# Latent and context attention of an even layer: two stages or one

## What is computed

```python
def diff_attend(q, k, v, lam):
    s = jnp.einsum('bhmqd,bhmkd->bhmqk', q, k).astype(F32) * (DIFF_DQK ** -0.5)
    p = jax.nn.softmax(s, axis=-1)
    p = p[:, :, 0] - lam * p[:, :, 1]
    return jnp.einsum('bhqk,bhkv->bhqv', p.astype(v.dtype), v)
```

## Time and profile before

| | |
|---|---|
| median of 3 runs | 4137.01 us (4134.11 to 4137.23) |
| profiled execution, its time | 4135.23 us |
| its span in the profile | 4133.4 us |
| TensorE busy | 3705.0 us, 90% of the span |
| VectorE busy | 2066.0 us, 50% |
| ScalarE busy | 872.8 us, 21% |
| GpSimd busy | 1419.3 us, 34% |
| mean granted TensorE clock | 0.945 of full |
| latent attention stage | from 358.6 us of the span |
| context attention stage | to 519.8 us |

### The profile page before, as it was taken

How to read it: one execution, slowest core, us unless ns; L and a number is a source line. 1 busy time by engine, 2 the same in 40 slices (tenths; PEclk the granted TensorE clock), 3 DMA queues, 4 the chain that set the end, 5 groups by cost and what they waited for, 6 DMA issues and landing times. The chain is left out here.

```text
span 4133.4 us, 45791 instructions
## 1 busy us (share of the span) xinstructions
PE 3705.0 (90%) x18442; PEld 2960.2 (72%) x18442; DVE 2066.0 (50%) x3080; ACT 872.8 (21%) x1697; POOL 1419.3 (34%) x612
## 2 busy tenths in 40 slices
PE   7897889999989889968999888888999888888998
PEld 3773467888878688857878466767888566777887
DVE  5796443223456366673233377763133477753132
ACT  2214312100021333301100343511000243511001
POOL 2321043235553100015455222245445222334454
PEclk9998789999999999989999899999999899999999
DMA  4534212212222000012332221123322321213332
GB/s 163 162 124 174 77 41 75 64 53 65 67 57 82 29 1 1 38 53 76 97 95 72 74 71 46 39 74 87 97 88 70 85 57 46 62 52 97 97 92 72
DMA packets 400351, 306.80 MB, mean 74 GB/s; under 512 B 11228, under 2 KB 367782, under 8 KB 399559
## 3 DMA queue, kind: packets, MB, share of 16 engines
q1 hardware_dynamic: 398040, 303.37, 24.4%
q10 hardware_dynamic: 2095, 0.44, 0.1%
HBM read 297.48 MB, written 6.29 MB: 73 GB/s over the span
## 5 line engine op out<-in xcount | busy, mean ns | idle before, releaser
L410 POOL TENSOR_TENSOR low<-raw,high 128x1024 fp32r<-128x1024 f32 (+1 forms) x437 | 1064.7, 2438 | 1437.3 <-DVE high L331 1437.3
L470 PE MATMUL scores<-high 128*128 128x512 f32 (+1 forms) x2464 | 949.2, 385 | 109.0 <-POOL low L410 82.6
L470 PE MATMUL scores<-low,high 128*128 128x512 f32 (+1 forms) x2464 | 935.2, 380 | 0.0
L470 PE MATMUL scores<-high,low 128*128 128x512 f32 (+1 forms) x2464 | 933.4, 379 | 0.0
L331 DVE CAST high<-raw 128x1024 fp32r<-128x1024 f32 (+1 forms) x437 | 414.3, 949 | 691.0 <-PE scores L470 375.9
L470 PE MATMUL bank<-high 128*128 128x512 f32 (+1 forms) x1792 | 666.7, 372 | 36.8 <-POOL low L410 26.9
L470 PE MATMUL bank<-low,high 128*128 128x512 f32 (+1 forms) x1792 | 663.5, 370 | 0.0
L470 PE MATMUL bank<-high,low 128*128 128x512 f32 (+1 forms) x1792 | 662.5, 370 | 0.0
L470 PEld LDWEIGHTS scores<-high 128*128 128x128 f32 x2464 | 475.8, 193 | 211.2 <-POOL low L410 87.8
L470 PEld LDWEIGHTS scores<-high,low 128*128 128x128 f32 x2464 | 473.9, 192 | 88.5
L470 PEld LDWEIGHTS scores<-low,high 128*128 128x128 f32 x2464 | 475.8, 193 | 84.4 <-issue 0.5
(11 more groups left out here) (581 smaller groups left out, 4358.6 us busy)
## 6 DMA issues: line engine op xcount, KB each, us to landing
raw<-in_mlp_w SPq DMA_DIRECT2D x128, 512.0 KB, 4.0
raw<-in_w_in SPq DMA_DIRECT2D x76, 512.0 KB, 3.9
ring<-in_ada_w SPq DMA_DIRECT2D x32, 1024.0 KB, 7.3
raw<-in_w_gate SPq DMA_DIRECT2D x44, 512.0 KB, 4.0
raw<-in_w_up SPq DMA_DIRECT2D x44, 512.0 KB, 3.9
raw<-in_w_down SPq DMA_DIRECT2D x40, 512.0 KB, 3.5
mix<-in_ada_w SPq DMA_DIRECT2D x16, 1024.0 KB, 7.1
raw<-in_od_w_in SPq DMA_DIRECT2D x29, 512.0 KB, 3.9
```

The lines of the kernel that those rows point to most:

```text
L410: pool.tensor_tensor(tile(low, u), tile(raw, u), tile(high, u).bitcast(F32), ALU.subtract)\
L470: mm = pe.matmul(out(p), stationary, moving, start=(k0 + k == 0 and i == 0), stop=(k0 + k == job.kc - 1 and i == len(pairs) - 1))
```

## The change

Both stages become one. Its units are L0 L1 C0 L2 L3 C1 ... L14 L15 C7: a context block behind every second latent block, 24 in all, with the loop order of before (scores one unit ahead, turn one unit behind) over this list. Context weights have tiles of their own (`p_ctx`, `pT_ctx`). The banks are divided anew: latent scores 0 to 3 as before; latent turns in 4 and in the first half of 5; context turns in the second half of 5; both maps of the context scores in bank 6, half each, where the second map's scores wait until the first's are done. The output products of both kinds go to bank 7, which they share with the modulation's products: an output waits until `flat` has been taken, and the modulation's next product waits until the output has been stored. Outputs are due two units after a head's last block. A context block's maxima are taken and scaled in one instruction each for both maps.

The side runs in the latent units only. Units 0 to 11 multiply as before. Unit 12 does nothing; units 13, 14 and 15 each turn four chunks of `flat` (16 products, 32 records) into bank 7, and VectorE adds the bias after each (three times in all). `LaterTurn` is gone. The 24 loads, their queue, their ring and their waits are unchanged.

The core of the diff (where "..." stands in `diff_attention`, the old code was that printed above; everything new is shown):

```diff
--- before.py
+++ after.py
@@ -936,11 +936,6 @@
 class LaterModulation(Modulation):
 
 
-    SIGNALS = Modulation.SIGNALS[:5]
-    TURN_SIGNALS = ("mod_turned", "mod_done")
-
-    def with_signals(self, signals):
-        *self.loaded, self.multiplied, self.taken = signals
 
     def take(self, act, n):
         act.wait_ge(self.multiplied, 2 * n + 2)
@@ -950,48 +945,42 @@
         for n in range(len(self.steps)):
             self.load(sp, n)
 
+    def wait_for_bank(self, pe, blocks):
+
+        n_units = len(self.steps)
+        if blocks:
+            pe.wait_ge(self.taken, min(blocks, n_units))
+        if blocks > n_units + 1:
+            pe.wait_ge(self.done, blocks - n_units - 1)
+
+    def units_of(self, u):
+        n = 4 * (u - len(self.steps) - 1)
+        return range(n, n + 4) if n >= 0 else range(0)
+
+    def outs(self):
+        return self.m.bank[self.banks[0]][:, 0:32].rearrange("p (i s) -> p i s", s=2)
+
     def tensor(self, pe, u):
         if u < len(self.steps):
             self.multiply(pe, u)
+        elif u > len(self.steps):
+            self.wait_for_bank(pe, u)
+            for n in self.units_of(u):
+                for i in range(4):
+                    mm = pe.matmul(self.outs()[:, 4 * (n % 4) + i, :], self.flat[:, n, i * P:(i + 1) * P], self.m.chosen,
+                                   start=True, stop=True)
+            mm.then_inc(self.turned, 1)
 
     def scalar(self, act, u):
         if u < len(self.steps):
             self.take(act, u)
 
     def vector(self, dve, u):
-        pass
-
-
-class LaterTurn:
-
-
-    SIGNALS = LaterModulation.TURN_SIGNALS
...
-            bias = self.m.ada_b[:, self.layer, 0:4 * self.units].unsqueeze(2).broadcast_to([P, 4 * self.units, 2])
-            dve.tensor_tensor(self.mods[:, 0:4 * self.units, :], self.out, bias, ALU.add).then_inc(self.done, 1)
+        if u > len(self.steps):
+            layer, at = self.steps[0][0], slice(4 * self.units_of(u)[0], 4 * self.units_of(u)[-1] + 4)
+            bias = self.m.ada_b[:, layer, at].unsqueeze(2).broadcast_to([P, 16, 2])
+            dve.wait_ge(self.turned, u - len(self.steps))
+            dve.tensor_tensor(self.mods[layer][:, at, :], self.outs(), bias, ALU.add).then_inc(self.done, 1)
 
 
 class FilterSpectra:
@@ -1362,143 +1351,179 @@
                                                   in1=small.norm_g[:, 0, :], op0=ALU.add, op1=ALU.mult))
 
 
-def diff_attention(nc, m, q, k, v, neg_lam, o, queries, keys, side=None):
-
-
-
-    q0, qn = queries
-    k0, kn = keys
-    nq, nk = qn // P, kn // P
+class HeadUnit:
+
+
+
+    def __init__(self, m, latent, n):
+        self.latent, self.n = latent, n
+        self.blocks = (LAT if latent else CTX)[1] // P
+        self.h, self.b = divmod(n, self.blocks)
+        self.q0, self.qn = LAT if latent else CTX
+        self.k0, self.kn = (0, TA) if latent else CTX
+        if latent:
+            self.score_parts = [[(m.bank[2 * mp], 0, 512), (m.bank[2 * mp + 1][:, 0:TC], 512, TC)] for mp in range(2)]
+            self.scores = [m.score[:, mp * 1024:mp * 1024 + TA] for mp in range(2)]
+            self.turned = [(m.bank[4], 0, 4), (m.bank[5][:, 0:2 * P], 4, 2)]
+        else:
+            self.scores = [m.bank[6][:, mp * TC:(mp + 1) * TC] for mp in range(2)]
+            self.score_parts = [[(self.scores[mp], 0, TC)] for mp in range(2)]
+            self.turned = [(m.bank[5][:, 2 * P:4 * P], 0, 2)]
+        self.last = self.b == self.blocks - 1
+
+
+def diff_attention(nc, m, q, k, v, neg_lam, o, side):
+
+
     scale = 64 ** -0.5
-    units = [(h, b) for h in range(HEADS) for b in range(nq)]
-    with buffers(nc, p=[P, 3, 2, TA], pT=[P, 2, NT, T], mx=[P, 2, 2], nb=[P, 2, 2], den=[P, 2, 2],
-                 r=[P, 2, 2]) as \
-            (p, pT, mx, nb, den, r), \
+    units = []
+    for n in range(HEADS * T // P):
+        units.append(HeadUnit(m, True, n))
+        if n % 2:
+            units.append(HeadUnit(m, False, n // 2))
+    where = {(x.latent, x.n): s for s, x in enumerate(units)}
+    earlier = lambda x, n: where.get((x.latent, x.n - n))
+    heads = [(s + 2, x) for s, x in enumerate(units) if x.last]
+    due = lambda step: [x for at, x in heads if at == step or (step == len(units) and at > step)]
+    turn_of_output = {(x.latent, x.h): i + 1 for i, (_, x) in enumerate(heads)}
+
+    with buffers(nc, p_lat=[P, 3, 2, TA], p_ctx=[P, 3, 2, TC], pT_lat=[P, 2, NT, T], pT_ctx=[P, 2, TC // P, TC],
+                 mx=[P, 2, 2], nb=[P, 2, 2], den=[P, 2, 2], r=[P, 2, 2]) as \
+            (p_lat, p_ctx, pT_lat, pT_ctx, mx, nb, den, r), \
             stage(nc, "scored", "maxed", "raised", "mixed", "turned", "copied", "summed", "stored", "chain",
-                  *(side.SIGNALS if side else ())) \
+                  *side.SIGNALS) \
             as (block, scored, maxed, raised, mixed, turned, copied, summed, stored, chain, *side_signals):
...
+        side.with_signals(side_signals)
+        weights = lambda x: (p_lat if x.latent else p_ctx)[:, x.n % 3, :, :]
+        turned_weights = lambda x: (pT_lat if x.latent else pT_ctx)[:, x.h % 2, :, :]
+
+        @block.sync
+        def _(sp):
+            side.sync(sp)
 
         @block.tensor
         def _(pe):
...
+            def score(s):
+                x = units[s]
                 for mp in range(2):
...
+                    lo, same = 64 * mp, earlier(x, 1)
+                    if same is not None:
+                        pe.wait_ge(raised, 2 * same + (1 + mp if x.latent else 2))
+                    if mp and not x.latent:
+                        pe.wait_ge(scored, 2 * s + 1)
+                    for out, kk, n in x.score_parts[mp]:
+                        mm = pe.matmul(out, q[lo:lo + 64, x.h, x.q0 + x.b * P:x.q0 + (x.b + 1) * P],
+                                       k[lo:lo + 64, x.h, x.k0 + kk:x.k0 + kk + n], start=True, stop=True)
                     mm.then_inc(scored, 1)
 
...
+            def turn(s):
+                x = units[s]
+                pe.wait_ge(mixed, s + 1)
+                if s:
+                    pe.wait_ge(copied, 2 * s)
+                for bank, first, n in x.turned:
+                    for i in range(n):
+                        tr = pe.transpose(bank[:, i * P:(i + 1) * P],
+                                          weights(x)[:, 0, (first + i) * P:(first + i + 1) * P], m.ident[:, :])
                 tr.then_inc(turned, 1)
 
...
+            def output(x, n_side):
+                nth = turn_of_output[(x.latent, x.h)]
+                pe.wait_ge(copied, 2 * (where[(x.latent, x.n)] + 1))
+                if nth > 1:
+                    pe.wait_ge(stored, nth - 1)
+                side.wait_for_bank(pe, n_side)
+                for i in range(x.kn // P):
+                    mm = pe.matmul(m.bank[7][:, 0:x.qn], v[:, x.k0 // P + i, x.h * P:(x.h + 1) * P],
+                                   turned_weights(x)[:, i, 0:x.qn], start=(i == 0), stop=(i == x.kn // P - 1))
                 mm.then_inc(summed, 1)
 
             score(0)
...
+            for s in range(len(units) + 1):
+                if s + 1 < len(units):
+                    score(s + 1)
+                n_side = len([x for x in units[0:s] if x.latent])
+                if s < len(units):
+                    for x in due(s):
+                        output(x, n_side)
+                if s < len(units) and units[s].latent:
+                    n_stored = len([x for at, x in heads if at <= s])
+                    if n_stored:
+                        pe.wait_ge(stored, n_stored)
+                    side.tensor(pe, units[s].n)
+                if s >= 1:
+                    turn(s - 1)
+            for x in due(len(units)):
+                output(x, HEADS * T // P)
 
         @block.scalar
         def _(act):
...
+            def raise_(s):
+                x = units[s]
                 for mp in range(2):
...
+                    act.wait_ge(maxed, 2 * s + mp + 1)
+                    if x.n >= 3 and mp == 0:
+                        act.wait_ge(turned, earlier(x, 3) + 1)
+                    act.activation(weights(x)[:, mp, :], x.scores[mp], ACT.Exp, bias=nb[:, s % 2, mp:mp + 1],
+                                   scale=scale, accum_out=den[:, s % 2, mp:mp + 1]).then_inc(raised, 1)
+
+            def copy(s):
+                x = units[s]
+                if x.b == 0 and x.h >= 2:
+                    act.wait_ge(summed, turn_of_output[(x.latent, x.h - 2)])
+                act.wait_ge(turned, s + 1)
+                for bank, first, n in x.turned:
+                    act.activation(turned_weights(x)[:, first:first + n, x.b * P:(x.b + 1) * P],
+                                   bank[:, 0:n * P].rearrange("p (i q) -> p i q", q=P), ACT.Copy)\
+                        .then_inc(copied, 2 // len(x.turned))
+
+            def store(x):
+                act.wait_ge(summed, turn_of_output[(x.latent, x.h)])
```

(58 more changed lines are left out.)

95 lines of the change are left out of this document (removed).

## The result

| | before | after |
|---|---|---|
| median | 4137.01 us | 4153.48 us |
| lowest to highest of 5 runs | 4134.11 to 4137.90 | 4148.84 to 4159.27 |
| ratio to before, 95% interval | | 1.0047 (1.0036 to 1.0058) |
| span of the profiled execution | 4133.4 us | 4147.1 us |

The change makes the kernel slower by 16 us. The forecast had been +5, at most +15 (4152).

A forecast was written before the change was run, and what follows sets the result against it. Attention bound by ada_w loads, then TensorE, at half clock in the context stage. 24.5 us later at L13, tail 57 instead of 78.3 (+3.2), dip +2.6, head norm -1: +5, median 4142 us, range 4127 to 4152.

The forecast's parts named there:

- The walk up to L13: TensorE steps from scores of L3 to L13: five pairs at full clock, 85.8 us; L13's scores 24.5 us later.
- the pairs with outputs: Two latent blocks and a context block, with head outputs and stores sharing bank 7: 21.3 us instead of 14.4.
- the ring's latency: Second ada_w half of a pair's second latent block waits for its load; with that hidden, 12.5 us instead of 14.4.
- The serial context scores: Context block's two score maps in bank 6, one after the other: 1.2 us on TensorE, bounds 0.7 and 1.5.
- the term of the clock in the middle: Pairs before L13: TensorE idles 2 us per softmax chain, so one clock dip at an output product, +2.6 us.
- The tail: From scores of L13 to the last store: 45.2 us at full clock, 63.1 at half, 57 taken; before 78.3.
- the turn's three groups: 32 modulation turn records in each of L13, L14 and L15: 4.0 us at full clock, later groups above 6.5.
- The head norm at full clock (-1): Head norm behind the attention stage may begin at full instead of half clock: -1 us.
- The blocks hide as meant: Rival: load waits take up the context blocks, pairs near 12 to 12.5 us, result -10 to -20; chance 0.16.
- The slower rival: Tail of L13 to L15 stays at half clock: +9.3 us, with one or two dips +12 to +15; chance 0.34.
- S(L13) after 475: Sign of error: scores of latent block 13 start after 475 us, meaning dips or an unseen wait; forecast near 466.

The follow-up runs named there:

- fill: Changed kernel plus two unused 512-column TensorE products in each of the first six context steps, in the idle spot; 4135.38 us, ratio 0.9999.
- split: Changed kernel with the second ada_w half of every odd latent block multiplied one step later, in the context step; 4125.19 us, ratio 0.9978.
- turn_fill: Kernel before with one extra 512-column TensorE product in each of the context stage's eight units; 4138.00 us, ratio 1.0005.
- split_spread: As split, with the modulation's 48 two-column products spread, eight in each context step of C1 to C6, into bank 6; 4111.03 us, ratio 0.9941.
- the trace of both: As split_spread, turns in seven spots, plus output products in bank 6 and context outputs one step later; 4107.77 us, ratio 0.9933.

## Why the prediction was wrong

**The walk up to L13** held at full clock. Its step sum of 85.8 us was met to 0.1 us by the run with the idle spots filled, pair by pair, the pairs with outputs among them (21.2 for 21.3); the ring's latency (12.7 for 12.5) was met by the run that removed it. The serial context scores, put at 1.2 us between bounds of 0.7 and 1.5, took 1.44 on TensorE (389.11 to 390.55).

**The step that failed** is the term of the clock in the middle: "a dip as before at O [...] should come about once more: +2.6". It was 14.2 us in the first trace and 8.4 in the second, seven falls and four, and with the idle spots filled it was nothing. The price of one, about 2 us, was near enough to the 2.6; the number of them was wrong. The signs were in my own sentences: I had written 2 us of idle time into every chain step, and had before me the one place of before where such a step stands without a load product behind it (441.44 to 445.25), followed at once by the half-clock O of 8.06. I counted the event once because it stood there once, instead of asking how often it comes in each of the places of that kind that the change makes: five chain steps in the stretch and two waits for a store. The upper end of the range carried only two dips, and so was too low as well.

**The tail** held as a sum: 57 taken, 57.4 and 58.7 measured, with the turn's three groups at 18.1 us in all where full clock gives 12. There was luck in it, since 57 was a choice between 45 and 63, and its parts came in another order: the first group, forecast at full clock behind two outputs, took 6.34 us, and the second, forecast slow, 4.80. The sum of walk and tail without dips is +3.2 for the stage; with the measured 14.2 it is +17.4, and the stage took 18.2 more.

**The head norm at full clock (-1)** did not come about: its first 16 records, from 539.83 us, take 8.44 us, against 7.62 before.

**The rivals.** "The blocks hide as meant" did not happen: S(L13) at 481 instead of 455 or less. The slower rival named the tail; the tail's sum was as forecast, and the loss sits in the middle, again in the granted clock. What I had listed as a sign of error, S(L13) after 475, is what came.

The skill's clock rule has it that the throttled state is the default and activity releases it (the Trainium skill, "TensorE: Matmul & The Clock Gate", "What's actually happening"). It fits the pairs better than I allowed it: in fill and split, with the spots filled, the stretch is at 1.00. For the continuous two-column products the traces still contradict it (479.4 to 499.5 us of before, never idle and at 0.50).

So the change gives up the cover that it found. Before, the latent stage had idle time for loads, in waits of up to 1.9 us in front of ada_w products, and the clock stayed at 1.00; why it stays up there and falls behind 1.44 us in the pairs was not tested. The context blocks fill that time, the two M of a pair move together, and a bare softmax chain of 3.8 us is left in every third step. The same merge with one half of M moved into that spot is 24 to 28 us faster than without (4125 against 4149 and 4153), and 9 us faster than before (0.9978). Without the loads to hide behind it is a loss of 13 us (4111.9 against 4098.9).

## What to carry to other kernels

When an order is merged, walk it for idle spots too, not only for its length: count how many spots like the one after which the profile shows the clock fall the new order makes, and price each of them, with a range, since a second trace can show half as many falls. If a spot can't be avoided, put work that is needed anyway into it; here that, together with the load wait that it removed, turned a loss of 13 to 16 us into a gain of 9. A product that shares a bank with a store, and narrow products gathered at the end of a stage, are the next terms to take apart: worth some 9 to 11 and 14 to 15 us here (by the medians and by the ratios, 0.9978 against 0.9951 and 0.9941).

## What the runs showed of the hardware

- Extra, useless TensorE work made the changed kernel faster: two products of 512 columns in each of six idle spots, 13 to 18 us in the medians (4135.4 against 4148.7 and 4153.5; ratios 0.9999 against 1.0033 and 1.0047), with the granted clock of the stretch from 0.83 or 0.89 to 1.00.
- The same products ending 5 us ahead of the idle spot held the clock of the stretch at 0.98 too, with the 1.44 us of idle time still in place. An idle spot of that length alone does not decide: S(L9) in the second trace of the changed kernel, and S(L14) in the trace of turn_fill, run on at full clock behind one.
- Eight two-column products between other work ran at full clock (1.84 us) with no fall behind them in five places of split_spread; in the trace of both, one such group had M at 3.06 instead of 1.92 behind it. The same products in the context stage of before, with TensorE 100% busy, ran at 0.50 (3.57 us).
- Two profiled executions of the changed kernel differ in the granted clock of its pairs, 0.83 and 0.89, and with it in the length of that stretch by 5.8 us: the same program meets more or fewer of the falls.
